# Gated linear attention: the forward and the backward direction of one head on the two halves of the partitions

## The reference

```python
def gla_causal_chunked(q, k, v, log_a):
    bcum = jnp.cumsum(log_a..., axis=3)
    btot = bcum[:, :, :, -1:, :]
    q_dec = qc * jnp.exp(bcum)
    k_inv = kc * jnp.exp(-bcum)
    k_end = kc * jnp.exp(btot - bcum)
    att = jnp.where(mask, jnp.einsum('bhnid,bhnjd->bhnij', q_dec, k_inv), 0.0)
    o_intra = jnp.einsum('bhnij,bhnjv->bhniv', att, vc)
    kv_chunk = jnp.einsum('bhnjd,bhnjv->bhndv', k_end, vc)
    decay = jnp.exp(btot[:, :, :, 0, :])
    ...  # S = decay * S + kv_chunk, over the chunks; S_prev is S before a chunk
    o_inter = jnp.einsum('bhnid,bhndv->bhniv', q_dec, S_prev)
    return (o_intra + o_inter).reshape(B, H, T, dv)
...
    o_f = gla_causal_chunked(qh, kh, vh, gf)
    o_b = flip(gla_causal_chunked(flip(qh), flip(kh), flip(vh), flip(gb)))
    o = (o_f + o_b)[:, :, pad:, :].transpose(0, 2, 1, 3)
```

## Time and profile before

| | |
|---|---|
| median of 3 runs | 3768.78 us (3767.61 to 3772.61) |
| the profiled execution | 3774.64 us, its span 3772.7 us |
| PE busy | 3700.5 us, 98% of the span |
| VectorE busy | 2463.1 us, 65% |
| ScalarE busy | 1563.5 us, 41% |
| mean granted clock of TensorE | 0.991 |
| mixer of the second block, layer 0 | about 1707 to 1960 us |
| the same, layer 1 | about 2916 to 3173 us |

### The profile page before, as it was taken

One profiled execution on the slowest core, in us unless ns is written; L12 is line 12 of the kernel. 1 busy time (PEld: TensorE's weight loads), 2 busy tenths in 40 slices (PEclk: granted clock), 3 DMA queues, 4 the chain that ended last, 5 costly groups with the idle time before them and its releaser, 6 DMA issues.

```text
span 3772.7 us, 64110 instructions
## 1 busy us (share of the span) xinstructions
PE 3700.5 (98%) x24764; PEld 3356.0 (89%) x24764; DVE 2463.1 (65%) x3356; ACT 1563.5 (41%) x2643; POOL 800.2 (21%) x663
## 2 busy tenths in 40 slices
PE   8999999999999999999999999999999999999998
PEld 5777888677788889999998999999999999899998
DVE  4667763666776386774447586779667435759667
ACT  3544332354433254454233454445445313445444
POOL 1111110111111043330002053335322000305332
PEclk9999999999999999999999999999999999999999
DMA  3122223212222222322110232332233212022223
GB/s 115 46 68 78 94 97 103 82 43 71 74 97 96 101 84 96 107 90 88 57 62 23 73 99 96 104 105 86 98 101 105 68 51 68 12 96 90 93 99 107
DMA packets 106052, 313.32 MB, mean 83 GB/s; under 512 B 29920, under 2 KB 30048, under 8 KB 105536
## 3 DMA queue, kind: packets, MB, share of 16 engines
q1 hardware_dynamic: 105232, 304.60, 24.6%
q0 software_dynamic: 560, 5.09, 0.4%
HBM read 307.48 MB, written 2.10 MB: 82 GB/s over the span
## 4 chain that ended last, share of the span: by engine, by line
PE 87%; issue 5%; DVE 4%; POOL 2%; ACT 1%; DMA 0%; SPq 0%; DVEq 0%; POOLq 0%; ACTq 0%
PE acc L2483 35%; PE misc L2944 21%; PE acc L2965 14%; PE acc L2576 3%; PE misc L3307 1%; PE acc L2921 1%; PE acc L3289 1%; DVE w_lo L1771 1%; PE misc L2483 1%; PE acc L3021 1%; PE misc L3123 1%; POOL probs_hi L2307 1%; PE acc L2559 1%; PE misc L2502 1%; PE misc L3112 1%
## 5 line engine op out<-in xcount | busy, mean ns | idle before, releaser
L633 ACT CAST w_hi<-stage 128x1024 fp32r<-128x1024 f32 x308 | 321.8, 1045 | 793.0 <-PE acc L2483 663.9
L2483 PE MATMUL acc<-x_hi,w_hi 128*128 128x264 f32 (+1 forms) x2048 | 573.7, 331 | 4.3 <-DVE w_lo L1340 2.9
L2483 PE MATMUL acc<-x_lo,w_hi 128*128 128x264 f32 (+1 forms) x2048 | 569.2, 329 | 0.0
L2483 PE MATMUL acc<-x_hi,w_lo 128*128 128x264 f32 (+1 forms) x2048 | 567.3, 328 | 0.0
L1340 DVE TENSOR_TENSOR w_lo<-stage,w_hi 128x1024 fp32r<-128x1024 f32 x308 | 418.1, 1357 | 195.4 <-ACT w_hi L633 186.4
L1771 DVE TENSOR_TENSOR w_lo<-stage,w_hi 128x512 fp32r<-128x512 f32 (+1 forms) x432 | 389.9, 905 | 153.5 <-ACT w_hi L967 150.3
L967 ACT CAST w_hi<-stage 128x512 fp32r<-128x512 f32 (+1 forms) x432 | 261.0, 605 | 338.9 <-PE acc L2965 293.8
L2483 PEld LDWEIGHTS acc<-x_hi,w_hi 128*128 128x128 f32 x2048 | 348.9, 192 | 48.4 <-issue 9.5
L2483 PEld LDWEIGHTS acc<-x_lo,w_hi 128*128 128x128 f32 x2048 | 347.9, 191 | 33.3
L2483 PEld LDWEIGHTS acc<-x_hi,w_lo 128*128 128x128 f32 x2048 | 347.8, 191 | 32.7
L2944 PE MATMUL misc<-t_hi,w_hi 128*128 128x264 f32 x1280 | 367.1, 287 | 5.6 <-ACT p_part L988 3.3
(11 more groups left out here) (403 smaller groups left out, 8279.0 us busy)
## 6 DMA issues: line engine op xcount, KB each, us to landing
stage<-weights SPq DMA_DIRECT2D x568, 512.0 KB, 3.3
rotary_decay<-tables POOLq DMA_DIRECT2D x2, 2048.0 KB, 8.5
x<-x_in SPq DMA_DIRECT2D x4, 512.0 KB, 7.5
lse_rows<-lse_columns SPq DMA_DIRECT2D x128, 0.5 KB, 2.0
out<-x SPq DMA_DIRECT2D x8, 256.0 KB, 2.1
rotary_masks<-tables SPq DMA_DIRECT2D x2, 784.0 KB, 5.0
params<-params SPq DMA_DIRECT2D x2, 279.0 KB, 3.7
consts<-consts POOLq DMA_DIRECT2D x1, 529.0 KB, 4.7
```

The costliest lines, as they stand in the source:

```text
L633: nc.scalar.copy(whi[p][:, :], stage[p][:, :]).then_inc(hi_ready, 1)
L2483: ins = mm(ps[:, b, 0:tn], ww, act_[:, kt, t0:t0 + tn], start=start and n == 0 and q == 0, stop=stop and n == last and q == 2)
```

## The change

A tile of QD and KI now holds one head, its forward direction on partitions 0 to 63 and its backward direction on 64 to 127.

- `decayed` writes each half of the partitions apart, for two heads: eight instructions for four.
- `chunk_states` makes one product for each chunk and head with 128 key columns (both directions), contraction 64; the chunks alternate between the two halves of the token rows and between two PSUM banks. 18 products stand where 32 stood.
- `chunk_decays` takes one head with six instructions, since the two directions lie in different slots. `states` runs both directions of a head, each on its half of the partitions: 14 instructions for one head where 14 served two, and two of them share a step.
- `intra` is split into `forward` and `backward`, which waits for `forward` of the same group.
- `masked` adds the two directions' masked scores after the product with the masks; `intra_out` then makes one product for a tile where it made two.
- `inter_out` contracts over both directions at once: 9 products for 16.

```diff
                 def decayed(dm):
-                    mt = dm % 2
+                    d, mt = dm // 2, dm % 2
                     dve.wait_ge(e_ready, at(4, dm + 1))
...
+                    first, rest = (0, META) if d else (META - 1, META + 63)
+                    for h in range(2):
+                        r, w = slice(64 * h, 64 * h + 64), slice(64 * d, 64 * d + 64)
+                        nc.vector.scalar_tensor_tensor(QD[w, 2 * mt + h, :], QKO[r, mt, :], 0.125, E1[r, :], ALU.mult, ALU.mult)
+                        nc.vector.tensor_tensor(KI[w, 2 * mt + h, :], QKO[r, 2 + mt, :], E2[r, :], ALU.mult)
+                        nc.vector.tensor_copy(DC[w, 2 * mt + h, 0:1], E1[r, first:first + 1])
+                        ins = nc.vector.tensor_copy(DC[w, 2 * mt + h, 1:9], E1[r, rest:rest + 7 * 64 + 1:64])
+                    ins.then_inc(e_used, 1)
+
+                def chunk_decays(h):
+                    dve.wait_ge(kv_full, at(4, h + 1))
...
+                    lo, up = slice(0, 64), slice(64, P)
+
+                    def scaled(r, to, src, k, c, n):
+                        dec = DC[r, h, c:c + 2 * n - 1:2].unsqueeze(2).to_broadcast([64, n, P])
+                        return nc.vector.tensor_tensor(S[r, to:to + 2 * n - 1:2, :], src[r, k:k + n, :], dec, ALU.mult)
+
+                    scaled(lo, 2, odd, 0, 1, 3)
+                    scaled(lo, 0, odd, 3, 7, 1)
+                    scaled(lo, 3, even, 0, 2, 3)
+                    scaled(lo, 1, even, 3, 0, 1)
+                    scaled(up, 0, odd, 0, 1, 4)
+                    scaled(up, 1, even, 0, 2, 4).then_inc(kv_read, 1)
+
+                def states(h):
+                    dve.wait_ge(kv_read, at(4, h + 1))
+                    for k in range(7):
+                        for r, c, prev, dec in ((slice(0, 64), (k + 2) % 8, k + 1, k + 1), (slice(64, P), 6 - k, 7 - k, 7 - k)):
+                            ins = nc.vector.scalar_tensor_tensor(SS[r, h % 2, c * P:(c + 1) * P], SS[r, h % 2, prev * P:(prev + 1) * P],
+                                                                 DC[r, h, dec:dec + 1], SS[r, h % 2, c * P:(c + 1) * P],
+                                                                 ALU.mult, ALU.add)
+                            if k < 6:
+                                ins.then_inc(dve_step, 1)
+                        if k < 6:
+                            dve.wait_ge(dve_step, steps.up(2))
+                    ins.then_inc(state_ready, 1)
 
...
-                        ins = nc.vector.tensor_tensor(dst[:, 0:w], src[:, 0:w], mask[:, 0:w], ALU.mult)
+                        chain(nc.vector.tensor_tensor(dst[:, 0:w], src[:, 0:w], mask[:, 0:w], ALU.mult))
+                        both = ways(dst, w)
+                        ins = nc.vector.tensor_tensor(both[:, :, 0, :], both[:, :, 0, :], both[:, :, 1, :], ALU.add)
                     ins.then_inc(att_ready, 1)
...
+                def chunk_states(mt):
...
+
+                    def product(h, c):
                         t, n = (c + 1) // 2, chunks[c][1]
...
+                        r0 = 64 * ((c + 1) % 2) if c else 0
+                        r, w = slice(r0, r0 + n), slice(64 if c == 8 else 0, 64 if c == 0 else P)
+                        bank, k = (2 * (h % 2), (c - 1) // 2) if c % 2 else (2 * (h % 2) + 1, (c // 2 + 3) % 4)
+                        return mm(M[w, bank, k * P:(k + 1) * P], LG[r, t, h * P + w.start:h * P + w.stop],
+                                  VA[r, t, h * P:(h + 1) * P], start=True, stop=True)
+
+                    pair = (2 * mt, 2 * mt + 1)
+                    for h in pair:
+                        ins = product(h, 0)
+                    ins.then_inc(pe_step, 1)
+                    for h in pair:
+                        product(h, 1)
+                    pe.wait_ge(pe_step, pes.up())
+                    for h in pair:
+                        for c in (2, 3, 4, 5, 6, 7, 8):
+                            ins = product(h, c)
+                        ins.then_inc(kv_full, 1)
...
-                        for d in range(2):
-                            at0 = 256 * (t % 2) + d * P
-                            ins = mm(M[0:n, 2 + g % 2, at0:at0 + n], KI[r, 2 * d + mt, c0:c0 + n],
-                                     QD[r, 2 * d + mt, c0:c0 + n], start=True, stop=True)
-                    ins.then_inc(att_full, 1)
+                    one_way(h, g, 0).then_inc(pe_step, 1)
+
+                def backward(h, g):
+                    pe.wait_ge(pe_step, pes.up())
+                    one_way(h, g, 1).then_inc(att_full, 1)
+
+                def intra(h):
+                    forward(h, 0)
+                    forward(h, 1)
+                    backward(h, 0)
+                    backward(h, 1)
...
                     for t in range(2 * g, min(2 * g + 2, 5)):
                         c0, n = TILES2[t]
                         b, c = col(c0)
-                        for d in range(2):
-                            at0 = 256 * (t % 2) + d * P
-                            ins = mm(M[:, b, c:c + n], VA[0:n, t, h * P:(h + 1) * P], atg(k)[0:n, at0:at0 + n],
-                                     start=d == 0 and t in (0, 3), stop=False, skip_group_check=True)
+                        at0 = 256 * (t % 2)
+                        ins = mm(M[:, b, c:c + n], VA[0:n, t, h * P:(h + 1) * P], atg(k)[0:n, at0:at0 + n],
+                                 start=t in (0, 3), stop=False, skip_group_check=True)
                     ins.then_inc(go_used, 1)
 
                 def inter_out(h):
-                    mt, r = h // 2, slice(64 * (h % 2), 64 * (h % 2) + 64)
-                    pe.wait_ge(state_ready, at(4, 2 * mt + 2))
-                    for d in range(2):
-                        for s in range(8):
-                            c0, n = chunks[s + 1 - d]
-                            b, c = col(c0)
-                            ins = mm(M[:, b, c:c + n], SS[r, d, s * P:(s + 1) * P], QD[r, 2 * d + mt, c0:c0 + n],
-                                     start=False, stop=d == 1 and s == 7, skip_group_check=True)
+                    pe.wait_ge(state_ready, at(4, h + 1))
+                    for k in range(9):
+                        c0, n = chunks[k]
+                        b, c = col(c0)
+                        r, slot = slice(64 if k == 0 else 0, 64 if k == 8 else P), k % 8
+                        ins = mm(M[:, b, c:c + n], SS[r, h % 2, slot * P:(slot + 1) * P], QD[r, h, c0:c0 + n],
+                                 start=False, stop=k == 8, skip_group_check=True)
                     ins.then_inc(go_full, 1)
 
```

More of the change, by code:

```diff
@@ L2095, in mixer2 @@
                 strip_out(RA[:, 2, :])
-                chunk_decays(1, 0)
-                chunk_decays(1, 1)
+                chunk_decays(2)
+                chunk_decays(3)
                 split_lo()
-                states(1, 0)
+                states(2)
                 scale(3)
@@ L2102, in mixer2 @@
                 split_lo()
[L2103 removed]
+                states(3)
                 rope(3)
@@ new lines, in chunk_states, with one_way @@
+                    pair = (2 * mt, 2 * mt + 1)
[9 more added lines that the diff above has]
+                        ins.then_inc(kv_full, 1)
+                def one_way(h, g, d):
+                    r = slice(64 * d, 64 * d + 64)
+                    for t in range(2 * g, min(2 * g + 2, 5)):
+                        c0, n = TILES2[t]
+                        at0 = 256 * (t % 2) + d * P
+                        ins = mm(M[0:n, 2 + g % 2, at0:at0 + n], KI[r, h, c0:c0 + n], QD[r, h, c0:c0 + n], start=True, stop=True)
+                    return ins
@@ L3132, in head_square @@
                         pe.wait_ge(q_sin, at(5, 5))
-                    rows(acc[1], ones128, QD[:, 2 * (h % 2) + h // 2, :]).then_inc(g_ms, 1)
+                    rows(acc[1], ones128, QD[:, h, :]).then_inc(g_ms, 1)
                 def mean_square(i):
@@ L3176, in mixer2 @@
                 intra_out(0, 0)
-                intra(0, 2)
+                forward(0, 2)
                 intra_out(0, 1)
+                backward(0, 2)
                 strip_of()
@@ L3187, in mixer2 @@
                 intra_out(1, 0)
-                intra(1, 2)
+                forward(1, 2)
                 intra_out(1, 1)
+                backward(1, 2)
                 strip_of()
@@ L3206, in mixer2 @@
                 intra_out(2, 0)
-                intra(2, 2)
+                forward(2, 2)
                 intra_out(2, 1)
+                backward(2, 2)
                 strip_of()
@@ L3217, in mixer2 @@
                 intra_out(3, 0)
-                intra(3, 2)
+                forward(3, 2)
                 intra_out(3, 1)
+                backward(3, 2)
                 strip_of()
```

95 lines of the change are left out of this document (24 added, 71 removed).

## The result

The changed kernel takes 3781.67 us (median of 8 runs, 3778.54 to 3784.13), the kernel before 3771.7 us beside it (8 runs, 3767.61 to 3779.08): a ratio of 1.0020, interval 1.0011 to 1.0029. It is slower by 10 us, where 3756.0 was forecast. The profiled execution took 3782.84 us with a span of 3781.0 and a mean granted clock of 0.990; before it was 3774.64, 3772.7 and 0.991.

The account below looks back on a forecast made before the run. It took PE, 98% busy, as the bound, with VectorE's reserves deciding the stalls. From 3774.64 us it took 7.6 (PE's 11.0 less 7.2 of stalls, both layers) and 11 of clock: 3756.0 us, range 3744 to 3768.

Parts of the forecast that it names:

- PE's own work: PE, mainly `inter_out` (6.5 us) and `intra_out` with the third `intra` group (4.7): 11.0 us less in a layer.
- stalls: PE waiting for VectorE at the recurrences: 3.1 us at the first pair of heads, 3.9 at the second, 7.2 a layer.
- clock in the GLA parts, falls behind stalls included: Slow clock over the mixer: 20.5 us lost today, 2.5 left and 7 new behind stalls, net 11 us won.
- a step becomes 0.27 + 0.387 = 0.65 us: `states` on VectorE: a step's second instruction starts 0.27 us after the first; 4.5 us a head, range 2.67 to 5.4.
- the strip behind the second, where 0.2 was: Strip after the second stall: late by 0.7 us, of which the cover leaves 0.2 us of waiting.
- the low end and the value taken: `chunk_states` on PE: low end 0.124 us a product (-1.4 us), taken 0.232 us (4.1 us in all, +0.1 twice).
- the rule by columns: Skill rule that a weight load costs by columns, not rows: 18 loads of 128 columns exceed 32 of 64.
- I expect most of the falls behind `inter_out` to go, with 2.5 us left.: Clock behind `inter_out`: with the group at 2.1 us instead of 3.71, 2.5 of 20.5 us of loss stay.
- The price of a stall ("about 2 us"): Slow clock behind four stalls of 3.1 to 3.9 us: about 2 us each, one perhaps without, 7 us together.
- The two places of the stalls: PE waits for the strip's evacuation at the first pair of heads and for `scale` at the second.
- `decayed`, `masked` and `split_lo` hidden: VectorE: `decayed` 1.45 us longer each time, `masked` 0.3 to 0.4, `split_lo` in time for its strip; PE loses nothing.
- Rival 3: VectorE bounds the four recurrences, `states` running serially at 5.4 us; stalls 22 us, clock not won back; 3784 us, chance 11%.

Follow-up runs that it names:

- spread versions: Changed kernel with recurrences cut into pieces placed in VectorE's idle stretches, `scale(3)` moved ahead of the third `chunk_decays`; two orders: 3749.14 us, then 3746.04 us (again 3747.71).

## Why the prediction was wrong

Both layers together. PE's own work is summed from the rows of layer 0 below, the rest are means of three profiles each, with spans of 3774.3 us before and 3780.5 after:

| term | predicted | measured |
|---|---|---|
| PE's own work | −22.0 | −16.4 |
| stalls | +14.4 | +20.1 |
| clock in the GLA parts, falls behind stalls included | −11 | −3.4 |
| slow clock in the attention parts | 0 | +5.8 |
| sum | −18.6 | +6.1 (spans: +6.2) |

The clock's line is by the granted clock. The first three lines make +0.3 us, and by their lengths the GLA parts of the two kernels differ by 0.2. The unprofiled runs of before lie some us under its profiled ones, and those of the changed kernel hardly; so the medians differ by 10 us.

- **The step that failed first: `states`, "a step becomes 0.27 + 0.387 = 0.65 us".** It is 0.754 us, because an instruction on the other half of the partitions doesn't start early, and the 0.27 was read from instructions that all have the same 128 partitions. The trace of before had a nearer row: `k_lo`, four instructions of 64 partitions and 528 elements that alternate, shown below. 5.28 us for a head is the high end that stood in the range; `chunk_decays` took 2.74 for 2.6. The stalls came out at 4.7 and 5.6 us for 3.1 and 3.9, and nothing at the strip behind the second, where 0.2 was: 20.1 us for 14.4. Of the 1.6 us by which the first is longer, `states` has 0.8, `chunk_decays` with a gap between its two heads 0.3, and 0.5 is what PE gained at `chunk_states` and then only waited. In VectorE's timeline of before, layer 0 (x4 in 2.87 us is 0.72 apart, one after the other; at 1746.05 `q_decayed`, 128 partitions wide, takes 0.71 us and the instruction behind it starts 0.62 us later):

```profile
1936.02 2.87 DVE L2029 TENSOR_TENSOR k_lo_twice<-qkv,k_hi_twice 64x528 fp32r<-64x528 f32 x4 [1.23 <-ACT k_hi_twice L1142]
```

- **PE's saving.** In a layer: `inter_out` 4 × (3.71 − 2.39) = 5.3 for 6.5, since the 64-row products at its ends cost 0.43 together; `intra_out` with the third group of `intra` 4 × (2.91 − 2.21) = 2.8, and the last `intra_out` 0.9, for 4.7; `intra` of two groups 2.01 where it was 1.72 to 1.79, −1.1 for 0; strips behind a 64-row product 6.05 for 5.86, −0.7 for 0; `chunk_states` 3.47 us for 3.99, +1.0 for −0.2. That makes 8.2 us a layer for 11.0. `chunk_states` is between the low end and the value taken, 0.193 us a product where products on one half of the rows took 0.232. This fits the overlap of loads on other row groups in the Trainium skill (TensorE: Matmul & The Clock Gate, "The mechanism"), which the prediction set against the rule by columns; no run changed the order of the halves alone, so it is not shown to be the cause. In PE's timeline of the changed kernel:

```profile
1788.52 3.54 PE L3087 MATMUL misc<-va_tokens,log_gates 16*64 16x128 f32 x36
```

- **The clock, the term with the largest error (7.6 us): "I expect most of the falls behind `inter_out` to go, with 2.5 us left."** Take, in the chains of waits of the two first profiles, what each row takes beyond its time at the full clock. Before this is 18.2 us, where the prediction had 20.5 to win back. In the changed kernel it is 13.8: 6.0 behind `inter_out`, where 2.5 stood, and 7.8 behind the stalls, where 7 stood. So the change is −4.4 by this count and −3.4 by the granted clock, for −11. The price of a stall ("about 2 us") held. What failed is the cause of the falls behind `inter_out`: a shorter group was to be enough, and the 64-row products at its ends have no place in the prediction. With them and the stalls 10 of 24 groups have a fall, with them alone 5 of 24, and with 128 rows throughout none of 16, stalls or not. Three of these falls are in the first profile: the strip of 8.35 us, 32 us behind the first stall, and in layer 1 those of 7.59 and 7.29 us, for 6.05; the 8.04 and 7.38 us there stand right behind the stalls.
- **A term that was not there: the attention parts.** 5.8 us of slow clock came in behind the GLA, where the instructions are the same and the prediction counts nothing. Their cause stays open.
- **What held.** The two places of the stalls, their releasers, `decayed`, `masked` and `split_lo` hidden, the doubled `decayed` leaving 1.64 us of its 3.12 us of idle time. Rival 3 (3784 us) gave the right sign by the right mechanism, serial steps, and its stalls of 22.0 us are near the 20.6 measured. That its time is near the measured one is in part luck: it took PE's saving for 22.0 us where it is 16.4, and 9.6 us more of slow clock where 2.4 came in all.

## What to carry to other kernels

Don't put two dependence chains on the two halves of the partitions to hide one's latency behind the other's: for 128 elements the pair took 0.754 us where two steps of one chain on all partitions take 0.774, so nothing overlaps and each chain merely has half the width. What PE saves is paid out only while its suppliers' reserve in that stretch lasts; the same instructions moved into the idle stretches turned +10 us into about −25, and keeping every product of a group on the same rows gave 10 more. Price a wait of PE of 5 us at its length and a third to a half again in slow clock: here 20.6 us of waiting cost 27.5 us on 128 rows and 31.6 with 64-row products, while eight waits of 1.3 to 2.7 us had no fall behind them.

## What the runs showed of the hardware

- VectorE: 14 independent instructions of 64x128 are 0.362 us from start to start when they alternate between the partition halves and 0.272 when they change once.
- PE: nine products of 64 columns take 1.96 us when all use 128 rows and 2.39 when the first and the last use 64; a strip behind a 64-row product takes 6.05 us and one behind a 128-row product 5.91 to 5.93. Behind the groups of 1.96 us the clock never fell (16 of them), behind those of 2.39 us it did in 15 of 48 (changed and spread versions, six profiles).
- PE: 18 products with weight loads of 128 columns that alternate between the row halves take 3.47 us, 0.193 each, where products with 128 columns of weights on all rows took 0.273.
- After the same wait in the same instructions the granted clock stays low for a time that differs from profile to profile: the 32 attention parts of sixteen profiles took 190.1 to 190.3, 190.7 to 191.2, 192.7 to 193.0 or 194.2 to 194.3 us. What chooses among the four stays open.
